# Three low parts on GpSimd's queue, each two row gathers later

## The reference, cut to what matters

```python
q = (xc @ w_query).reshape(C, PEER_HEADS, 2, PEER_HALF)      # 8 heads, 2 halves of 128
sc = jnp.einsum('thpd,hpnd->thpn', q, sub_keys)              # 128 scores a half
top_s, top_i = lax.top_k(sc, PEER_TOPK)                      # 16 best of each half
best_s, best_pos = lax.top_k(cand_s, PEER_TOPK)              # 16 best of the 256 pairs
u = expert_down[experts]; vv = expert_up[experts]            # gathered rows
act = jax.nn.gelu(jnp.einsum('cd,chkd->chk', xc, u), approximate=False)
w = gates * act                                              # gates: softmax of best_s
out = jnp.einsum('chk,chkd->cd', w, vv)
```

## Time and profile before

| | us |
|---|---|
| three runs | 1365.88, 1366.78, 1370.14 |
| median | 1366.78 |
| profiled execution, its own time | 1370.13 |
| its span in the profile | 1368.3 |
| TensorE busy | 1230.3 |
| VectorE busy | 764.4 |
| ScalarE busy | 613.7 |
| GpSimd busy | 877.1 |
| mean rate of the DMA engines | 293 GB/s |
| chain that ended last: DMA | 24% |
| chain that ended last: TensorE | 54% |

### The profile page before, as it was taken

The page is one execution under the profiler, slowest core; times in us unless marked ns, Lnnn a source line. Parts: engine busy times, 40 slices in busy tenths (PEclk is TensorE's granted clock), DMA queues, the critical chain, the costliest instruction groups (busy, mean ns, idle before and its releaser), DMA issues.

```text
span 1368.3 us, 17435 instructions
## 1 busy us (share of the span) xinstructions
PE 1230.3 (90%) x5976; PEld 875.9 (64%) x5976; DVE 764.4 (56%) x1573; ACT 613.7 (45%) x1303; POOL 877.1 (64%) x533
## 2 busy tenths in 40 slices
PE   8999988988888886777787898999999999999997
PEld 6878864444444442333233344789999988899886
DVE  6945497777778767777667654703582422222101
ACT  6576544433443442332323323446465455555432
POOL 5735766655766646554444442797978874788995
PEclk9999999999999999899998899999999999999999
DMA  7632599999999999999999997464646653555562
GB/s 270 201 106 81 201 398 390 426 427 426 427 424 426 424 428 425 427 426 427 427 427 413 415 427 294 158 212 143 189 136 177 223 157 123 170 186 186 187 205 96
DMA packets 72945, 400.64 MB, mean 293 GB/s; under 512 B 8097, under 2 KB 8353, under 8 KB 39713
## 3 DMA queue, kind: packets, MB, share of 16 engines
q0 software_dynamic: 36864, 268.45, 46.9%
q1 hardware_dynamic: 33696, 123.35, 27.9%
q10 hardware_dynamic: 2304, 7.79, 1.6%
HBM read 396.42 MB, written 3.15 MB: 292 GB/s over the span
## 4 chain that ended last, share of the span: by engine, by line
PE 54%; DMA 24%; DVE 9%; POOL 6%; ACT 4%; issue 3%; ACTq 0%; POOLq 0%; SPq 0%; DVEq 0%
DMA arena<-in_experts,arena 23%; PE bank L602 13%; PE bank L603 12%; PE bank L604 12%; PE bank L920 11%; POOL w_lo L1467 5%; DVE arena L1846 3%; PE bank L667 1%; ACT arena L1249 1%; POOL arena L1511 1%; ACT diag L1255 1%; PE bank L658 1%; PE bank L1044 1%; PE bank L1030 1%; DMA ring<-in_stream 0%
## 5 line engine op out<-in xcount | busy, mean ns | idle before, releaser
L1467 POOL TENSOR_TENSOR w_lo<-ring,w_hi 128x1024 fp32r<-128x1024 f32 x222 | 551.9, 2506 | 169.7 <-ACT w_hi L1073 169.3
L920 PE MATMUL bank<-arena,diag 128*128 128x512 f32 x968 | 459.1, 625 | 92.8 <-ACT diag L1255 92.3
L1511 POOL DMA_INDIRECT arena<-in_experts,arena x242 | 287.2, 1187 | 238.9 <-PE bank L920 155.4
L1846 DVE CUSTOM_DVE_ANT_0 arena<-arena 128x1024 f32<-128x1024 f32 x242 | 321.1, 1338 | 163.3 <-DMA arena<-in_experts,arena 162.0
L920 PEld LDWEIGHTS bank<-arena,diag 128*128 128x128 f32 x968 | 186.1, 199 | 345.7 <-issue 207.7
L1073 ACT ACTIVATE w_hi<-ring 128x1024 fp32r<-128x1024 f32 x228 | 239.8, 1057 | 146.8 <-PE bank L604 113.7
L602 PE MATMUL bank<-hT_hi,w_hi 128*128 128x256 f32 x736 | 209.0, 284 | 3.2 <-DVE hT_lo L1549 2.7
L604 PE MATMUL bank<-hT_hi,w_lo 128*128 128x256 f32 x736 | 205.3, 279 | 0.0
L603 PE MATMUL bank<-hT_lo,w_hi 128*128 128x256 f32 x736 | 205.3, 279 | 0.0
L1246 ACT ACTIVATE arena<-arena 128x2 f32<-128x2 f32 (+2 forms) x99 | 20.2, 204 | 408.7 <-DVE arena L1846 408.6
L602 PEld LDWEIGHTS bank<-hT_hi,w_hi 128*128 128x128 f32 x736 | 139.6, 190 | 8.3 <-issue 7.3
(11 more groups left out here) (265 smaller groups left out, 1615.3 us busy)
## 6 DMA issues: line engine op xcount, KB each, us to landing
ring<-in_stream SPq DMA_DIRECT2D x228, 512.0 KB, 3.7
arena<-in_experts,arena POOLq DMA_INDIRECT x242, 13.6
kv_park<-arena ACTq DMA_DIRECT2D x8, 256.0 KB
arena<-kv_park ACTq DMA_DIRECT2D x1, 2048.0 KB, 7.7
x_res<-in_x SPq DMA_DIRECT2D x2, 512.0 KB, 4.8
arena<-in_mem SPq DMA_DIRECT2D x1, 1024.0 KB, 11.0
arena<-in_sub_keys ACTq DMA_DIRECT2D x1, 1024.0 KB, 5.5
out<-arena SPq DMA_DIRECT2D x2, 512.0 KB, 2.6
```

The costliest lines, as they stand in the source:

```text
L920: mm = pe.matmul(y_banks[half][:, :], diag[:, slot % DIAGS, :], rows_buf[BUFFER[slot]][:, D + 512 * half:D + 512 * half + 512], start=(i = ...
L1467: nc.gpsimd.tensor_tensor(w_part(w_lo_mem, c), ring[:, c % RING, :], w_part(w_hi_mem, c).bitcast(F32), ALU.subtract).then_inc(S("lo_made"), 1)
L1511: nc.gpsimd.indirect_dma_start(out=rows_buf[b], out_offset=None, in_=experts, in_offset=bass.IndirectOffsetOnAxis(ap=expert_u[:, slot:slot ...
L1846: v.tensor_tensor_reduce(out=rows_buf[b][:, 0:D], in0=xn[:, slot // (PEER_H * PEER_K), :], in1=rows_buf[b][:, 0:D], scale=1.0, scalar=0.0, ...
```

## The change

One line: the three entries that were put in by hand stand at the slots 3, 5 and 7 in place of 1, 3 and 5.

```diff
 LOW_AT = {max(at - 2, 8): i for i, at in enumerate(CHUNK_AT)}
-LOW_AT.update({1: -3, 3: -2, 5: -1})
+LOW_AT.update({3: -3, 5: -2, 7: -1})
```

## The result

| | before | after |
|---|---|---|
| median of 7 runs each, side by side | 1370.14 (1365.88 to 1371.42) | 1374.49 (1370.82 to 1375.75) |
| ratio | | 1.0032 (1.0019 to 1.0044) |
| profiled execution, its own time | 1370.13 | 1375.02 |
| its span | 1368.3 | 1373.2 |

The changed kernel is slower by 4.4 us, with an interval of 2.6 to 6.0. Repeated later beside 35 runs of the kernel before (median 1370.04) it took 1371.63 in 11 runs, ratio 1.0020 (1.0008 to 1.0032), that is 1.1 to 4.4 us. The ratios are those on record; they are not exactly the quotients of the two medians (here 1.0012). One of the 35 took 1742.98 us at a granted clock of 0.66 and is left out of the ratio. Two things stand out at once: it lost what was forecast or somewhat more, and the three runs shown ahead of the prediction had put the median of the kernel before 3.4 us too low.

A forecast was written before the change was run, and what follows sets the result against it. The row gathers were taken as DMA bound, so the change was judged on its start: VectorE's chain makes the product of slot 6 +2.4 us late, which on the median of 1366.78 gives 1369.2 us; range 1364.0 to 1373.5 us.

The forecast's parts named there:

- the two free casts: VectorE's casts at 168.59 and 187.51 no longer held by low parts: -1.8 and -2.15 us.
- two held instructions behind 191 us: VectorE, due at 190.8: gate argument and dot of slot 3 run into low parts 44 and 45, dot +2.4 us.
- The forecast loss of +2.4: TensorE's product of slot 6 goes from 206.60 to 209.0 by VectorE's chain; the DMA bound stage moves with it.
- the last one of the sum: Adding +2.4 us to the median of 1366.78 us, giving 1369.2 us for the whole kernel.
- The bounds +0.95 and +3.3: Ends for the product of slot 6: +0.95 by TensorE alone, +3.3 if gather 8's delay decides.
- The sum 3.3 - 2.35: TensorE up to slot 6: its later start less idle time in waits for diagonals, giving +0.95 us.
- The wait for low part 43: TensorE at chunk 43, starting about 183.4: a wait of over 2 us for that low part.
- I count nothing for it: TensorE's granted clock, 1.00 in these stretches with keep-busy products ahead of slot 0: no term in the sum.
- A: Dot of slot 1 wins against low part 43, making chunk 43 4.3 us late: +5.3 us, 1372.1 us; chance 0.20.
- B: Full DMA rate 2.3 us sooner is kept, the path through chunk 43 has slack: -2.3 us, 1364.5 us; chance 0.16.
- C: Buffers' round trip sets gathers 8 to 15 and shifts cancel: 0, 1366.8 us; chance 0.12.
- The rule that I had weighed: VectorE and GpSimd's shared ports: first issuer holds the lock; the dot at 180.8 would hold low part 43.

The follow-up runs named there:

- an edit that made the first product 2 us earlier: Low parts 41, 42, 43 put ahead of gathers 1, 2, 3, against the kernel before: 1371.97 us, ratio 1.0023 (1.0011 to 1.0034).
- the eight extra products: 20 keep-busy products in place of 12 ahead of the first row product, against the kernel before: 1370.02 us, ratio 1.0006 (0.9995 to 1.0017).
- the kernel with early gathers: Low parts 41 and 42 put ahead of gather 3, 43 left ahead of gather 5, against the kernel before: 1370.07 us, ratio 1.0006.
- entry 49 at 50: Low part ahead of gather 49 moved ahead of gather 50, against the changed kernel: 1373.65 us, ratio 1.0024 to the kernel before.

## Why the prediction was wrong, and where it was right

Right, by its own steps (0.69 us added to its times). Gather 1 at 169.09 (168.39 + 0.69 forecast); low part 43 from 181.71 (181.0 + 0.69); the first product at 194.40 (193.7 + 0.69) and gather 8 at 197.16 (196.5 + 0.69); the two free casts; the dot of slot 1 over 3 us long; two held instructions behind 191 us. The forecast loss of +2.4 measured +1.9 at the product of slot 6, and +1.7 to +2.8 at the dot of slot 24 in three executions with this order of the first slots. The mechanism of that term is the one forecast: the cast before is let go, and low parts 44 and 45 fall on the dot of slot 3 and what stands behind it. Both comparisons say slower, and the repeat's 1.1 to 4.4 us holds the 2.4.

**The step that failed** is the last one of the sum, the time to which the +2.4 was added: "on the median of 1366.78 that gives 1369.2 us". The profiled execution (1370.13) was the highest of the three runs, and I took the middle one for the kernel's time. With more runs the median of before is 1370.14 (7), 1370.04 (35), 1370.29 (31) and 1368.43 (29). The measured 1374.49 is 5.3 us above the forecast: 3.4 of them are this base, and the other 1.9 are the term of the change, +2.4 where the first comparison has +4.4. The base alone put the measured time outside the range: with 1370.14 its upper end would have been 1376.9. The chances were set on the same narrow ground. Their line between same and slower was drawn at 0.3% (4.1 us), from runs taken to lie "1 to 3 us apart". The first comparison's 1.0032 lies just above that line, the repeat's 1.0020 below it, and both intervals exclude 1.

**The size** of the term is in part open. The first comparison's interval begins at 2.6, just above the forecast, and the repeat is centred on 2.7. The table has the time 0.2 to 2.0 us above dot 4's shift in all eleven rows. Rows of one comparison share the runs of the kernel before, and each shift is of one execution, so a part of that may be error in common; no single wait in the traces accounts for it. The repeat's trace, with +1.9 at dot 4 and +0.8 at the last dot, shows that between the start and the end of the rows more comes and goes from one execution to the next than was forecast for the whole.

**Steps that were wrong without deciding the time.**

- The bounds +0.95 and +3.3 came from TensorE's path and gather 8. With that path 3.1 us late and VectorE's chain untouched the time moves by +0.8 (-0.7 to +2.3) and dot 24 by +0.1. The time rules out the +3.3 and not the +0.95, but in the trace TensorE is only 0.1 us late at slot 7. The sum 3.3 - 2.35 was too large, as TensorE gave back more than its waits for diagonals; what the rest was the rows don't show. Of the two it is VectorE's chain that the time follows.
- The wait for low part 43 was to be over 2 us and was 1.22. TensorE had already waited 2.52 us for chunk 41, its granted clock had a mean of 0.83 in 170 to 180 us (1.00 in the kernel before), and chunk 41 took from 173.70 to 177.71, 4.01 us against 2.83, so that TensorE came to chunk 43 later. "I count nothing for it" was wrong as a statement on the clock and right for the sum, as the low part would have been awaited anyway.
- Between low parts 44 and 45 the dot of slot 3 got in (191.41, 3.04 us, ahead of 194.39), where the forecast had it held by both. That took 1.2 us off, as only the short step behind it waited for low part 45. The two low parts took 5.65 us in place of some 4.9, which put 0.8 us on. So +2.4 became +1.9.

**The rivals.** A wanted the dot of slot 1 to win against low part 43. The race was not run: the dot came to start 0.26 us behind the low part, and the price of A was not tried. The forecast had it 0.2 us ahead; it left out that the selection step ahead of that dot needs scores from ScalarE, for which VectorE waited 0.61 us (the row of 180.24). B, that the earlier gathers are kept as a gain, a gain of 2.3 us, is refuted by the kernel that has them and leaves low part 43 in place (+0.8, -1.0 to +2.7). C, that nothing lasts, is refuted by the first comparison and by the repeat. The rule that I had weighed is told under the last heading.

## What to carry to other kernels

Find the engine whose chain feeds the next stage, and count an order by what that chain's instructions meet on the port they share with another engine: here an edit that made the first product 2 us earlier lost 3 us, and its trace has two low parts moved onto a dot. Test a critical path by delaying it alone, as the eight extra products did; it cost one line and showed that a path 3 us late need not lose 3 us. And before a small effect is put on a median of three runs, ask how far apart the runs are: here they were 4.3 us apart, and the effect forecast was 2.4.

## What the runs showed of the hardware

**Who wins between VectorE and GpSimd.** The dot at 301.04 starts 0.38 us ahead of the low part at 301.42, is held, and ends at 304.86, its own 1.2 us behind the low part's end. In the kernel with early gathers it starts 0.70 us ahead and is not held; there it is the low part that takes 2.71 us in place of 2.35. GpSimd and then VectorE of that kernel:

```profile
301.37 2.71 POOL L1467 TENSOR_TENSOR w_lo<-ring,w_hi 128x1024 fp32r<-128x1024 f32 x1
```

```profile
300.67 1.21 DVE L1846 CUSTOM_DVE_ANT_0 arena<-arena 128x1024 f32<-128x1024 f32 x1
```

In all thirteen traces, from 160 to 320 us, the dots that start 0.02 to 0.60 us ahead of a low part are held until its end (3.46 to 4.04 us long, 5.84 through two), and those that start 0.65 to 1.00 us ahead are not (1.21 to 1.30 us), but for one: in the kernel with all three low parts ahead of gather 7 a dot with a lead of 0.28 us is not held (194.69, 1.22 us; low part at 194.97). The Trainium skill (SBUF — State Buffer, Who interferes with whom) gives the lock to whoever issues first; by the starts that the profile records these traces disagree, for leads up to 0.60 us.

**Two low parts back to back.** Sometimes VectorE gets in between (191.41 above, 3.04 us for a dot), sometimes it is held through both (4.67 us at 170.86, 5.84 us at 185.28). What decides it the runs do not tell.

**TensorE's clock after a wait.** Waits of 2.5, 4.5 and 4.7 us are in stretches whose granted clock is 0.83, 0.66 and 0.75 in the mean, between the levels of 1.2 and 2.4 GHz, where it was 1.00 in the same stretches of the kernel before. At the lower level the products of a chunk start 0.21 us apart in place of 0.11. In the kernel with low part 43 alone late, chunk 43 took 5.1 us behind its wait of 4.54, against 2.83:

```profile
180.00:190.00 10.00, 5.33 (x24) 5.13 (x24) 9.62 (x28) 0.83 (x2) 5.34 (x4) 0.66 1.02 426
```

**Traces differ far behind the change.** In the MLP of the second block (1190 to 1280 us) the same products take 281 ns in some traces and 276 in others, at a granted clock of 1.00 in both. Groups of this stretch, in the kernel before, and in the one with eight more products:

```profile
L602 PE MATMUL bank<-hT_hi,w_hi 128*128 128x256 f32 x236 | 66.3, 281 | 0.0
```

```profile
L602 PE MATMUL bank<-hT_hi,w_hi 128*128 128x256 f32 x235 | 64.9, 276 | 0.0
```

From the start of the last dot to the end the first takes 520.4 us and the second 517.0. With entry 49 at 50 the changed kernel has 276 (517.9), an edit that lies 900 us earlier. Whether this goes with the execution or with the program is not shown, since the one kernel that was traced twice, the changed one, has 281 both times (521.2 and 520.5). What speaks for the execution: the seven traces with 276 are each among the three fastest of the 11 or 12 runs of their kernel, and the six with 281 or 282 stand at the fourth place or behind. If it went with the program instead, some 3.5 us of a comparison could come from it, which is as much as the change.

It is also not all that parts two runs of one kernel. The two executions of the changed kernel are 3.8 us apart (spans 1373.2 and 1369.4): 0.5 ahead of gather 0, 2.6 from there to the last dot, and 0.7 behind. This is why a profiled execution's own time is compared part by part here and not as a whole.
